# A permuted scratch layout for the state-space input, new orders in attention, and two norm sums placed elsewhere

## The reference

```python
x = x + 0.5 * swiglu(rms_norm(x, ff1_norm), ...)          # 1024 -> 2816 -> 1024
h = rms_norm(x, mix_norm)
q, k, v, u = split(h @ w_in)                               # 512, 128, 128, 512 columns
attn = banded_sink_attention(q, k, v, sink)                # 8 heads of 64, window 128, chunks of 64
bu = einsum('blgh,gph->blgp', u as (32 groups, 16), b_bar) # 64 complex states for each group
y = Re(C . scan(lam_bar, bu)) + D * u
z = gelu(y);  ssm = z * sigmoid(z @ w_glu + b_glu)
x = x + concat(rms_norm(attn), rms_norm(ssm)) @ w_out
x = x + 0.5 * swiglu(rms_norm(x, ff2_norm), ...)
out = rms_norm(x, final_norm)
```

## Time and profile before

| | |
|---|---|
| median of three runs | 1642.5 us (1642.36 to 1643.0) |
| the profiled execution, its own time | 1642.36 us |
| its span in the trace | 1640.7 us |
| TensorE busy | 1603.0 us (98%), 7540 matmuls |
| weight loads, VectorE, ScalarE, GpSimd busy | 80%, 67%, 43%, 32% |
| granted clock of TensorE, mean | 0.993 of full |

### The profile page before, as it was taken

One profiled execution on the slowest core, in us unless ns is written; L12 is line 12 of the kernel. 1 busy time (PEld: TensorE's weight loads), 2 busy tenths in 40 slices (PEclk: granted clock), 3 DMA queues, 4 the chain that ended last, 5 costly groups with the idle time before them and its releaser, 6 DMA issues.

```text
span 1640.7 us, 22012 instructions
## 1 busy us (share of the span) xinstructions
PE 1603.0 (98%) x7540; PEld 1316.5 (80%) x7540; DVE 1093.9 (67%) x1722; ACT 712.7 (43%) x1311; POOL 530.9 (32%) x953
## 2 busy tenths in 40 slices
PE   7999999999999999998999999999999999999998
PEld 5778888888888887877877778788888888888886
DVE  5866667766579887662358777765566666587765
ACT  6443443333334445521557544533433443344452
POOL 4004788877777777432030060000000000000011
PEclk8999999999999999999999999999999999999998
DMA  6345333443487545775431132233333333885443
GB/s 213 119 112 108 113 114 131 137 141 134 167 320 251 155 114 142 253 193 126 91 128 27 39 103 90 91 103 107 127 126 103 103 103 122 302 275 147 122 110 122
DMA packets 151032, 229.01 MB, mean 140 GB/s; under 512 B 18449, under 2 KB 87697, under 8 KB 147345
## 3 DMA queue, kind: packets, MB, share of 16 engines
q1 hardware_dynamic: 147856, 220.04, 41.8%
q0 software_dynamic: 3072, 7.62, 2.5%
HBM read 153.47 MB, written 74.15 MB: 139 GB/s over the span
## 4 chain that ended last, share of the span: by engine, by line
PE 57%; POOL 25%; issue 6%; DVE 5%; DMA 3%; ACT 2%; POOLq 1%; SPq 0%; DVEq 0%; ACTq 0%
PE bank L1135 18%; PE bank L1136 17%; PE bank L1137 17%; POOL pw L2958 2%; POOL EBb L3146 2%; POOL ptmp L3144 2%; POOL ptmp L3145 2%; POOL EBb L3160 2%; POOL ptmp L3159 2%; POOL ptmp L3158 2%; POOL ptmp L3104 1%; POOL ptmp L3102 1%; POOL cl_st L3108 1%; DMA par<-in_log_dt_dram 1%; DVE hblo L2296 1%
## 5 line engine op out<-in xcount | busy, mean ns | idle before, releaser
L1135 PE MATMUL bank<-hbhi,ws_lo 128*128 128x512 f32 x1056 | 413.9, 392 | 8.9 <-DVE ws_lo L2260 4.8
L1136 PE MATMUL bank<-hblo,ws_hi 128*128 128x512 f32 x1056 | 411.7, 390 | 0.0
L1137 PE MATMUL bank<-hbhi,ws_hi 128*128 128x512 f32 x1056 | 411.7, 390 | 0.0
L1135 PEld LDWEIGHTS bank<-hbhi,ws_lo 128*128 128x128 f32 x1056 | 198.8, 188 | 55.6 <-DVE ws_lo L2260 6.4
L2859 POOL TENSOR_TENSOR ssq<-ssq,sqt 128x512 f32<-128x512 f32 x25 | 34.8, 1392 | 643.5 <-ACT sqt L1661 641.3
L1135 PE MATMUL bank<-d_hi,ws_lo 128*128 128x512 f32 x616 | 240.6, 391 | 0.0
L1137 PE MATMUL bank<-d_hi,ws_hi 128*128 128x512 f32 x616 | 239.7, 389 | 0.0
L1136 PE MATMUL bank<-d_lo,ws_hi 128*128 128x512 f32 x616 | 239.7, 389 | 0.0
L1136 PEld LDWEIGHTS bank<-hblo,ws_hi 128*128 128x128 f32 x1056 | 198.8, 188 | 41.4 <-issue 0.5
L1137 PEld LDWEIGHTS bank<-hbhi,ws_hi 128*128 128x128 f32 x1056 | 198.8, 188 | 41.4
L1729 ACT ACTIVATE loc<-bank 128x512 f32<-128x512 f32 x160 | 95.6, 597 | 254.9 <-PE bank L1137 254.9
(11 more groups left out here) (298 smaller groups left out, 2620.9 us busy)
## 6 DMA issues: line engine op xcount, KB each, us to landing
b_scratch<-loc SPq DMA_DIRECT2D x42, 1024.0 KB, 7.3
d_in<-b_scratch SPq DMA_DIRECT2D x154, 256.0 KB, 3.2
raw2a<-in_ff_w_up_dram SPq DMA_DIRECT2D x44, 512.0 KB, 4.9
loc<-in_ff_w_gate_dram SPq DMA_DIRECT2D x36, 512.0 KB, 4.7
xT<-x_scratch SPq DMA_DIRECT2D x12, 1024.0 KB, 7.3
x_scratch<-xT SPq DMA_DIRECT2D x5, 2048.0 KB, 8.3
dw_lo_place<-in_ff_w_down_dram SPq DMA_DIRECT2D x8, 1024.0 KB, 7.4
x_in<-in_x_dram SPq DMA_DIRECT2D x8, 512.0 KB, 6.8
```

What stands on the lines that cost most here:

```text
L1135: nc.tensor.matmul(o, wl, rh, start=first, stop=False, skip_group_check=chain)
L1136: nc.tensor.matmul(o, wh, rl, start=False, stop=False, skip_group_check=chain)
L1137: return nc.tensor.matmul(o, wh, rh, start=False, stop=last, skip_group_check=chain)
```

## The change

Four things are edited.

1. u goes through DRAM in another layout. The scratch is now (4, T, P, NC), `store_u` writes for each partition eight pieces of 512 bytes (before: one of 4 KB), and `load_u8` is one DMA with 4 KB for each partition (before: eight DMAs with 512-byte pieces). For that the 128 channels of a u unit leave the projection in the order (h, g) in place of (g, h): the two splits of units 0 to 3 write their tiles through the view `turned` and read `raw` through `natural`.
2. `norm_sum(N_MIX, 1)` moves from the middle of project o = 1 to between o = 0 and o = 1. `norm_spread(N_MIX, 1)` stays behind o = 1.
3. The orders of the attention stage on TensorE, ScalarE and VectorE are others. The steps are the same.
4. `norm_sum(N_FF2, 0)` moves from the middle of part 9 to behind part 8; the spread stays behind part 9.

```diff
--- before.py
+++ after.py
@@ -120,7 +120,7 @@
 IN_BANK = [1, 3, 5] + [(o + 1) % 2 for o in range(3, N_FIRST)] + [2, 3, 1, 0]
 
 
-WITH_PE = {(1, 1): steps("m1"), (4, 0): steps("E0 E1 E2 E3"), (5, 0): steps("E4 E5 E6 E7"), (6, 0): steps("K0"), (6, 1): steps("I0"),
+WITH_PE = {(4, 0): steps("E0 E1 E2 E3"), (5, 0): steps("E4 E5 E6 E7"), (6, 0): steps("K0"), (6, 1): steps("I0"),
            (7, 0): steps("I1 K1"), (7, 1): steps("I2"), (8, 0): steps("K2"), (8, 1): steps("K3"), (9, 0): steps("I3"),
            (9, 1): steps("Y0"), (10, 1): steps("Y1"), (11, 1): steps("Y2"), (12, 0): steps("Y3"),
            (13, 1): steps("v0 v1 v2 v3")}
@@ -137,11 +137,10 @@
 GATED_DVE = [("G", 0), ("G", 1), ("G", 2), ("G", 3), ("W", 11), ("G", 4), ("G", 5), ("G", 6), ("G", 7), ("W", 12), ("R", 0), ("R", 1)]
 
 
-ATT_PE = steps("S0 p0 S1 p1 S2 p2 T0 p3 T1 V0 S3 p4 V1 S4 T2 p5 T3 V2 S5 p6 V3 S6 p7 T4 p8 T5 V4 S7 p9 V5 p10 T6 p11 T7 V6 V7"
+ATT_PE = steps("S0 p0 S1 p1 S2 p2 T0 p3 V0 S3 T1 p4 V1 S4 T2 p5 V2 S5 T3 p6 V3 S6 T4 p7 V4 S7 T5 p8 V5 T6 p9 V6 p10 T7 p11 V7"
                " p12 p13 n0 n1 p14 r0 p15")
-ATT_ACT = steps("X0 X1 C0 W13 X2 C1 O0 X3 O1 C2 W14 X4 C3 O2 X5 O3 W15 C4 X6 C5 O4 s0 s1 X7 O5 C6 s2 s3 C7 O6 W16 O7 s4 s5 s6 s7"
-                " W17 n0 n1 h0 h1 h2 h3 W18 h4 h5 h6 h7 W19")
-ATT_DVE = steps("A0 p0 A1 B0 p1 B1 A2 W13 p2 A3 p3 B2 p4 B3 A4 W14 p5 A5 p6 B4 p7 B5 A6 W15 p8 A7 B6 p9 B7 p10 a0 W16 p11"
+ATT_ACT = steps("X0 X1 C0 W13 X2 O0 W14 C1 X3 O1 C2 X4 O2 W15 C3 X5 O3 C4 X6 O4 s0 s1 C5 X7 O5 s2 s3 C6 O6 W16 C7 O7 s4 s5 s6 s7 W17 n0 n1 h0 h1 h2 h3 W18 h4 h5 h6 h7 W19")
+ATT_DVE = steps("A0 p0 A1 B0 p1 p2 A2 W13 B1 p3 W14 A3 B2 p4 A4 B3 W15 p5 A5 B4 p6 A6 B5 p7 A7 B6 p8 a0 B7 p9 p10 W16 p11"
                 " a1 p12 W17 p13 n0 p14 h0 h1 h2 h3 p15 W18 n1 h4 h5 h6 h7 W19")
 
 
@@ -588,6 +587,13 @@
 
         return w_hi[slot_of(u)], w_lo[slot_of(u)]
 
+    def natural(t):
+        return t.rearrange("p (k g h) -> p k g h", g=8, h=GH)
+
+    def turned(t):
+
+        return t.rearrange("p (k h g) -> p k g h", g=8, h=GH)
+
     def a_block(n, kh, f):
 
         w, j = divmod(n, N_INST)
@@ -616,7 +622,7 @@
 
     bank = [ctx.enter_context(nc.psum_tensor(f"bank{i}", [P, HALF], F32)) for i in range(8)]
 
-    u_d = nc.dram_tensor("u_scratch", (DS, T, NC), F32, kind="Internal").ap()
+    u_d = nc.dram_tensor("u_scratch", (4, T, P, NC), F32, kind="Internal").ap()
     y_d = nc.dram_tensor("y_scratch", (DS, T, NC), F32, kind="Internal").ap()
     eb_d = nc.dram_tensor("eb_scratch", (P, 2, NJ, P), F32, kind="Internal").ap()
     cs_d = nc.dram_tensor("cs_scratch", (P, 2, NJ, NC), F32, kind="Internal").ap()
@@ -991,11 +997,9 @@
             for u in range(RS):
                 load_in(u)
 
-        u_v = u_d.rearrange("(g h) t c -> t h g c", h=GH)
-
         def store_u(i):
             sp.wait_ge(proj_taken, END_IN[i])
-            sp.dma_start(u_d[i * P:(i + 1) * P, :, :], ust[i % 3][:, :, :]).then_inc(u_stored, 16)
+            sp.dma_start(u_d[i].rearrange("t p c -> p t c"), ust[i % 3][:, :, :]).then_inc(u_stored, 16)
 
         def load_u8(i):
             sp.wait_ge(u_stored, 16 * (i + 1))
@@ -1003,9 +1007,9 @@
                 sp.wait_ge(x_parked, 48)
                 sp.wait_ge(h_tmp, 2 * KD)
             else:
-                sp.wait_ge(u8_loaded, 16 * T * i)
-            for t in range(T):
-                sp.dma_start(u8[t * GH:(t + 1) * GH, 8 * i:8 * i + 8, :], u_v[t][:, 8 * i:8 * i + 8]).then_inc(u8_loaded, 16)
+                sp.wait_ge(u8_loaded, 16 * i)
+            sp.dma_start(u8[:, 8 * i:8 * i + 8, :],
+                         u_d[i].rearrange("t (h g) c -> (t h) g c", g=8)).then_inc(u8_loaded, 16)
 
         def load_csn(b):
             sp.wait_ge(e_ready, 4 if b == 0 else 8)
@@ -1310,6 +1314,15 @@
                                                c_in[:, ri, i, :, :].rearrange("p a s -> p (a s)"), ident[:, :])
                 last.then_inc(ct_ready, 1)
 
+        def second_half(norm):
+
+            def between(n):
+                if n == 0:
+                    norm_sum(norm, 1)
+                elif n == 1:
+                    norm_spread(norm, 1)
+            return between
+
         def first_half(norm):
 
             def after(what, n):
@@ -1402,7 +1415,7 @@
         def inject(b):
 
             pe.wait_ge(e_taken, 2 * b + 2)
-            pe.wait_ge(u8_loaded, 16 * T * (b + 1))
+            pe.wait_ge(u8_loaded, 16 * (b + 1))
             for ri in range(2):
                 round_free("I", b, ri)
                 for jj in range(4):
@@ -1505,7 +1518,7 @@
             last.then_inc(mix_out, 1)
 
         step = {"K": blocks_k, "E": transposes_e, "I": inject, "Y": outputs_y,
-                "S": scores, "T": transposes_p, "V": weighted, "v": windows_v, "p": ssm_piece, "m": lambda h: norm_sum(N_MIX, h), "n": lambda h: norm_sum(N_ATT, h),
+                "S": scores, "T": transposes_p, "V": weighted, "v": windows_v, "p": ssm_piece, "n": lambda h: norm_sum(N_ATT, h),
                 "r": lambda h: norm_spread(N_ATT, h)}
 
         for o in range(N_FIRST):
@@ -1523,8 +1536,7 @@
             tiles = {0: split_before(N_MIX), 3: split_before(N_MIX) + KD}.get(o)
             project(u, h, bank[IN_BANK[o]][:, :], range(KD), True, True, tiles,
                     lambda: [step[kind](b) for kind, b in WITH_PE.get((o, 1), ())]).then_inc(proj_out, 1)
-            if o == 1:
-                norm_spread(N_MIX, 1)
+            second_half(N_MIX)(o)
 
         def glu(o):
 
@@ -1596,11 +1608,10 @@
                 att_part(i, (k,))
         norm_spread(N_ATT, 1)
         for i in range(N_SSM_OUT):
-            if i == LAST_IN_0 + 2:
-                att_part(i, range(2))
+            att_part(i, (3,) if i < 3 else range(4)).then_inc(mix_out, 1)
+            if i == LAST_IN_0 + 1:
                 norm_sum(N_FF2, 0)
-            att_part(i, (3,) if i < 3 else range(2, 4) if i == LAST_IN_0 + 2 else range(4)).then_inc(mix_out, 1)
-            if i == LAST_IN_0 + 2:
+            elif i == LAST_IN_0 + 2:
                 norm_spread(N_FF2, 0)
 
         def out_tile(t):
@@ -1644,7 +1655,10 @@
             act.wait_ge(raw_loaded[u % RS], loads_until(u))
             for s, v in wait_out:
                 act.wait_ge(s, v)
-            act.activation(w_split(u)[0][:, :], raw[u % RS][:, :], ACT.Copy).then_inc(w_hi_done, 1)
+            hi, src = w_split(u)[0][:, :], raw[u % RS][:, :]
+            if u < U_K:
+                hi, src = turned(hi), natural(src)
+            act.activation(hi, src, ACT.Copy).then_inc(w_hi_done, 1)
 
         def square(norm, n, src, as_src=lambda v: v):
 
@@ -2171,7 +2185,10 @@
         def split_lo(u):
             dve.wait_ge(w_hi_done, u + 1)
             hi, lo = w_split(u)
-            dve.tensor_tensor(lo[:, :], raw[u % RS][:, :], hi[:, :].bitcast(F32), ALU.subtract).then_inc(w_lo_done, 1)
+            hi, lo, src = hi[:, :].bitcast(F32), lo[:, :], raw[u % RS][:, :]
+            if u < U_K:
+                hi, lo, src = turned(hi), turned(lo), natural(src)
+            dve.tensor_tensor(lo, src, hi, ALU.subtract).then_inc(w_lo_done, 1)
 
         def norm_rms(norm, h):
```

## The result

| | before | after |
|---|---|---|
| median of four runs each | 1642.43 us (1642.13 to 1643.0) | 1656.35 us (1654.59 to 1657.01) |
| the profiled execution, its own time | 1642.36 us | 1656.16 us |
| its span in the trace | 1640.7 us | 1654.5 us |
| granted clock of TensorE, mean | 0.993 | 0.988 |

The ratio is 1.0082 (95% interval 1.0067 to 1.0096): slower by 13.9 us in the medians, where 12.0 us were forecast. The matmuls and their number are the same.

A forecast was written before the change was run, and what follows sets the result against it. TensorE was taken as the bound, busy for 98% of the span, so only its waits count. The terms +7.8 - 0.8 + 4.4 + 0.6 = +12.0 us gave 1654.4 us, range 1646.5 to 1659.5.

The forecast's parts named there:

- parts 1 and 2: Strided splits of units 0 to 3, norm_sum(N_MIX, 1) moved earlier: wait 6.3 us, lost clock 1.5, together +7.8 us.
- part 3: u through DRAM ahead of inject(3): load gains 2.0 us, store loses 1.2, so -0.8 us; clock still falls.
- part 4: New attention orders, walked: 9.4 us of waits against 4.0, 1.0 back, so +4.4 us.
- part 5: norm_sum(N_FF2, 0) six matmuls earlier: a wait of 1.4 us, 0.7 already paid, so +0.6 us.
- clock term: TensorE's clock falling behind the wait ahead of o = 1: 1.5 us lost.
- load term: u8's eight loads made one, ahead of inject(3): 5.5 us down to 3.5, so -2.0 us.
- store term: u's last store ahead of inject(3), in 512-byte rows, lands in 4.3 us: +1.2 us.
- the w_in row: Trace row: a 512 KB w_in unit in 512-byte rows lands 4.5 us after issue; held against a 3.1 us store.
- (a): Splits of units 0 to 3: the strided write is free, parts 1 and 2 +2.2, sum +6.4, 1648.8; chance 0.14.
- (b): Hand-over of u worth far more: part 3 at -4.8 instead of -0.8, sum +8.0, 1650.4; chance 0.10.
- (c): Attention, S3 to V7: the new order gains, -3.8 in place of +4.4, 1646.2; chance 0.07, of which 0.03 faster.
- (d): All moves do nothing, TensorE's waits only change place: within 3 us of before; chance 0.03.

The follow-up runs named there:

- experiment 2: Kernel before with only u's new scratch layout, its single load and the strided splits: 1645.27 us against 1642.69, ratio 1.0015.
- experiment 4: Kernel after with plain splits of units 0 to 3, output not the block's: 1649.08 us against the kernel before's 1642.69, ratio 1.0045.
- experiment 7: experiment 2 with VectorE's four takes ahead of split_lo(1) and (2), ScalarE's squares 12 to 15 ahead of its second split: 1639.65 us against 1642.54, ratio 0.9981.
- 6: experiment 2 with the splits writing in order and reading raw with a 64-byte step: 1643.85 us against the kernel before's 1642.54, ratio 1.0007.
- experiment 9: Kernel after with the three attention orders of the kernel before: 1649.77 us against the kernel before's 1642.83, ratio 1.0045.
- 10: experiment 7 with the TensorE and ScalarE attention orders of Experiment 8 and another VectorE order, strided writes: 1638.00 us against 1642.83, ratio 0.9969.
- 11: The kernel of 10 with the strided reads of 6 in place of strided writes: 1637.22 us against the kernel before's 1642.83, ratio 0.9967.
- 1: Kernel before with the three new attention orders alone: 1648.39 us against 1642.69, ratio 1.0042.
- experiment 3: Kernel before with norm_sum(N_MIX, 1) moved between o = 0 and o = 1 and nothing else: 1645.91 us against 1642.69, ratio 1.0020.
- experiment 5: Kernel before with units 0 to 3 written with steps of 8, 16, 32 and 64 bytes, output not the block's: 1644.6 us in one execution.
- Experiment 8: Kernel before with the new attention orders, but splits W14 and W15 put back where they stood: 1643.96 us against 1642.54, ratio 1.0004.

## Why the prediction was right

The time, the side and the mechanisms were forecast; two terms came out larger and one smaller, all three mostly by TensorE's clock. That the total came so close, 13.9 for 12.0, is in part luck. The terms were off by +1.7, -2.8, +4.3 and -0.1, and 1.2 us that have nothing to do with the change went the other way. Of the loss in the profiled execution about 7.0 us are clock (3.6 + 5.1 less the 1.7 that the kernel before lost), for which the forecast had 1.5; the waits cost less than forecast.

| step | forecast | trace of the kernel after |
|---|---|---|
| parts 1 and 2 | +7.8 (wait 6.3, clock 1.5) | +9.5 (wait 5.93, clock 3.6) |
| part 3 | -0.8 | -3.6 (wait -1.95, clock -1.6) |
| part 4 | +4.4 (waits +5.4, 1.0 back) | +8.7 (waits +3.7, clock 5.1, 0.1 back) |
| part 5 | +0.6 | +0.5 |
| sum | +12.0 | +15.1, and 1.2 less ahead of o = 0 |

**Parts 1 and 2** went as written: splits of 2.15 to 2.22 us (forecast 2.2), adds ending 11.5 us after the start of o = 0 (forecast 681.4 - 669.65 = 11.75), a wait of 5.93 for 6.3. Experiments 2, 4 and 7 show each link: with the step and without the move 3.3 us of wait, with the move and without the step 2.0, and none where the takes don't stand behind the splits. Mis-sized was the clock term: "I take 1.5" measured 3.6, since I took the size of one fall from the row behind L1411 and the clock, which fell at 676.9 while TensorE still waited, stayed low from the end of the wait to about 687. In time: eleven matmuls at a pitch longer by 0.2 us, 0.35 on the one ahead of them, and 0.8 on the eight small ones make 3.4 of it.

**Part 3.** The load term was right (-2.0 forecast, 5.51 to 3.45 us). The store term was wrong: "I take 4.3" for the landing, a loss of 1.2. Its landing in the kernel after is 3.9, but it can't be read alone. Ahead of it stand the landing of the k store and the issue of eight Mt loads, and what one gives the other takes: from `store_k(1)` to the issue of u's load there are 10.35 us before and 10.46 after. Over the five kernels with the old layout it is 10.09 to 10.35, over the eight with the new one 10.07 to 10.76, so the 512-byte rows cost about 0.2 us. The wait of `inject(3)` is 2.3 to 3.0 us in all eight, 4.6 to 5.1 in the five: the term is -2.0. By the sentence of the Trainium skill that the prediction quoted (512 bytes are enough for line rate; DMA: Bandwidth & Descriptors, "Specifications") it would have been -2.0 too; the w_in row that I held against it was the worse guide. One step held to a hundredth: `store_k(1)` starts 46.48 us after the spread of the norm before and 46.47 after (46.47 to 46.81 in all thirteen profiled kernels), so nothing earlier in SyncE's queue matters, as was said.

**The clock behind `inject(3)`** was forecast to fall, and didn't. What the profiled executions show:

| kernel | wait ahead of `inject(3)` | us of full clock lost behind it |
|---|---|---|
| before | 4.6 | 1.71 |
| after | 2.66 | none |
| experiment 2 | 2.83 | 1.71 |
| 4 | 2.3 | 1.70 |
| 6 | 2.8 | 1.70 |
| 7 | 2.71 | none |
| 9 | 3.01 | 1.71 |
| 10 | 2.72 | 1.70 |
| 11 | 2.6 | none |
| 1, 3, 5, 8 | 4.6, 4.9, 4.6, 5.1 | 3.4 each |

The rows of 10 and 7 (2.72 and 2.71 us) have the two outcomes, so the length of the wait alone doesn't decide. Where the clock fell is known for the profiled execution alone. The mean granted clock is known for every execution: in experiments 3 and 7 the slower ones have the lower clock (experiment 7: 0.995 at 1637.3 us, 0.993 at 1641.0), so single executions of one kernel differ in their falls; among the kernel before's own executions, whose means differ by 0.002 at most, there is hardly such an order.

**Part 4.** The places were walked rightly: T1, T2, T4 and T6 wait 1.11, 1.99, 2.28 and 1.05 us (walked: T1 1.1, T2 2.1, T4 2.25), S6 waits 0.65 (1.1) and V6 0.47. V3, V5 and the n1 step wait less than walked, so the sum is 7.7 instead of 9.4, 3.7 over the kernel before's 4.0. (For n1 the walk had 0.9 "as now"; the kernel before shows 0.2 there, and so does the kernel after.) The 1.0 us that more pieces behind transposes were to give back is not seen: waits and clock together account for all but 0.1 us of the change of C in the kernel after and in experiments 1, 4 and 8. Experiment 8 shows the cause in both directions. What failed is the value taken for the clock: zero in the forecast, "once or twice" in the bound of +7.5, three falls of 1.71 us in the profiled execution. The kernels with the new orders had two, three and two falls between first Y and the spread; the seven with the old orders none in five and one in two. They are not all of one kind. Two in the kernel after stand behind T2 and T4, and one in experiments 1 and 4 behind T2. The last, at 939.7 in the kernel after, has no new wait ahead of it. It comes 0.6 us behind the eight small matmuls of n1, whose own wait is 0.16 us, and the last longer wait is 0.47 us at 922.7:

```profile
938.06 1.02 PE L1165 MATMUL bank<-ones,ssq_a 128*128 128x1 f32 x8 [0.16 <-DVE xT L2786]
```

The same fall, some 2 to 3 us after n0 begins, is in experiments 1, 2, 4, 7 and 8, of which 2 and 7 have the old orders, and is missing in the other seven kernels. So about 3.4 of the 5.1 us stand behind the walked waits; the other 1.7 can't be put down to them.

**Part 5**: the wait is 1.29 where 1.4 was forecast, the cost 0.5 in the kernel after and in experiment 4. In experiment 9 the clock fell behind it (969 to 974), and the stretch is 35.98 us, 1.7 more than before.

**The rivals.** (a), a free step, is refuted by experiment 5. (b) was nearer in effect than the forecast (-3.6, against its -4.8 and the -0.8 taken): half by a shorter chain, half by the clock. (c), an order that gains, was false of this one; experiments 10 and 11 show that one with -1.4 exists. (d) is refuted by experiment 3.

**Slips in the working**, none of which changes the forecast: against (d) it says that no wait behind 681 could be shortened by more than 1.6 us, where the one at 918.55 is 1.73; the middle between (a) and (c) is 1647.5, not 1646.5; and with a store of 5.5 us and a load of 3.5 the high end of part 3 is +0.4, not +0.9.

Left open: what makes the clock fall behind one 2.7 us wait and not behind another, and behind the two sums of attention's norm in six kernels of thirteen. And the price of part 5 alone was read from the trace only; no kernel had it by itself.
